# A 31 tap depthwise convolution split over three engines or over four

## The reference, cut to what matters

```python
def conformer_conv(h, w_pw1, b_pw1, w_dw, b_dw, ln_g, ln_b, w_pw2, b_pw2):
    a, gate = jnp.split(h @ w_pw1 + b_pw1, 2, axis=-1)
    y = a * jax.nn.sigmoid(gate)
    y = lax.conv_general_dilated(y, w_dw[:, None, :], window_strides=(1,),
                                 padding=[(CONV_K // 2, CONV_K // 2)],
                                 ...
                                 feature_group_count=CONV_W) + b_dw
    y = jax.nn.silu(layernorm(y, ln_g, ln_b))
    return y @ w_pw2 + b_pw2
```

## Time and profile before

| | |
|---|---|
| median of 3 executions | 3255.95 us (3248.94 to 3261.28) |
| the profiled execution | 3254.23 us |
| its span, first to last instruction | 3252.0 us |
| TensorE busy (matmul) | 2921.1 us, 90% |
| VectorE busy | 1574.0 us, 48% |
| ScalarE busy | 1086.2 us, 33% |
| GpSimd busy | 682.4 us, 21% |
| mean granted clock of TensorE | 0.908 of full speed |

### The profile page before, as it was taken

The page is one execution under the profiler, slowest core; times in us unless marked ns, Lnnn a source line. Parts: engine busy times, 40 slices in busy tenths (PEclk is TensorE's granted clock), DMA queues, the critical chain, the costliest instruction groups (busy, mean ns, idle before and its releaser), DMA issues. The chain is left out here.

```text
span 3252.0 us, 30964 instructions
## 1 busy us (share of the span) xinstructions
PE 2921.1 (90%) x12206; PEld 2206.4 (68%) x12206; DVE 1574.0 (48%) x2360; ACT 1086.2 (33%) x1578; POOL 682.4 (21%) x532
## 2 busy tenths in 40 slices
PE   6978589999999888899999897897999989899998
PEld 4855257888777633588887694355788866578886
DVE  5343536364342356364554425446555379743332
ACT  3222134343333334443334523333222231342223
POOL 6998910000000000000000000039995011000000
PEclk8975589999899889999998896788999899999999
DMA  5542212332212200123323230024554211123331
GB/s 165 165 144 93 85 58 78 97 98 89 67 60 72 78 1 1 52 85 97 97 88 101 76 97 13 1 65 136 170 173 136 72 52 60 44 74 96 97 97 52
DMA packets 284806, 274.66 MB, mean 84 GB/s; under 512 B 13473, under 2 KB 268727, under 8 KB 284407
## 3 DMA queue, kind: packets, MB, share of 16 engines
q1 hardware_dynamic: 266759, 210.47, 20.7%
q0 software_dynamic: 16864, 62.17, 5.8%
q10 hardware_dynamic: 1040, 0.07, 0.0%
HBM read 270.56 MB, written 2.10 MB: 84 GB/s over the span
## 5 line engine op out<-in xcount | busy, mean ns | idle before, releaser
L422 DVE TENSOR_TENSOR w_lo<-raw,w_hi 128x1024 fp32r<-128x1024 f32 x396 | 540.6, 1368 | 1110.8 <-ACT w_hi L418 1110.6
L1566 PE MATMUL G<-H_hi,w_hi 128*128 128x512 f32 (+1 forms) x2048 | 816.3, 399 | 84.6 <-DVE H_lo L330 37.4
L418 ACT ACTIVATE w_hi<-raw 128x1024 fp32r<-128x1024 f32 x396 | 418.4, 1057 | 1287.2 <-PE G L1566 1160.8
L1566 PE MATMUL G<-H_lo,w_hi 128*128 128x512 f32 (+1 forms) x2048 | 805.9, 393 | 0.0
L1566 PE MATMUL G<-H_hi,w_lo 128*128 128x512 f32 (+1 forms) x2048 | 805.1, 393 | 0.0
L1566 PEld LDWEIGHTS G<-H_hi,w_hi 128*128 128x128 f32 x2048 | 392.9, 192 | 185.6 <-issue 84.9
L1566 PEld LDWEIGHTS G<-H_lo,w_hi 128*128 128x128 f32 x2048 | 392.7, 192 | 83.4 <-issue 3.9
L1566 PEld LDWEIGHTS G<-H_hi,w_lo 128*128 128x128 f32 x2048 | 392.2, 191 | 81.9
L1566 PE MATMUL G<-hid_hi,w_hi 128*128 128x512 f32 x864 | 342.5, 396 | 4.6 <-DVE hid_lo L1227 3.9
L1566 PE MATMUL G<-hid_hi,w_lo 128*128 128x512 f32 x864 | 338.2, 391 | 0.0
L1566 PE MATMUL G<-hid_lo,w_hi 128*128 128x512 f32 x864 | 338.1, 391 | 0.0
(11 more groups left out here) (279 smaller groups left out, 3333.5 us busy)
## 6 DMA issues: line engine op xcount, KB each, us to landing
raw<-in_w_ff SPq DMA_DIRECT2D x128, 512.0 KB
mod_w<-in_w_mod POOLq DMA_DIRECT2D x112, 512.0 KB, 4.0
raw<-in_ffn_w_up SPq DMA_DIRECT2D x176, 256.0 KB
raw<-in_ffn_w_down SPq DMA_DIRECT2D x40, 512.0 KB
raw<-in_w_in SPq DMA_DIRECT2D x28, 512.0 KB
raw<-in_mlstm_w_in SPq DMA_DIRECT2D x24, 512.0 KB
raw<-in_kv_w SPq DMA_DIRECT2D x16, 512.0 KB
raw<-in_fox_w_qg SPq DMA_DIRECT2D x16, 512.0 KB
```

The lines of the kernel that those rows point to most:

```text
L418: act.activation(w_hi[:, j, :], raw[:, j, :], ACT.Copy).then_inc(hi_done, 1)
L422: dve.tensor_tensor(w_lo[:, j, :], raw[:, j, :], w_hi[:, j, :], ALU.subtract).then_inc(lo_done, 1)
L1566: mm = pe.matmul(G[:, 2 * p + m, 0:n], lw[:, k, ms], rh[:, t, 0:n], start=(t == 0 and q == 0), stop=(t == st["ktiles"] - 1 and q == 2), sk ...
```

## The change

TensorE keeps the last 7 of the 31 taps, VectorE the first 15. Nine taps, 15 to 23, are computed as products by ScalarE, `yp` times the tap's weight (a Copy with a scale per partition), into a ring of four tiles `tap_prod`; GpSimd adds the nine products of a group to `tap_sum` (a buffer of two) in eight chained additions. `total` on VectorE waits for these additions and adds `tap_sum` before it adds `M`. The diagonals of the next group are now built behind a group's additions.

```diff
-PE_TAPS = 10
-V_TAPS = CONV_K - PE_TAPS
+PE_TAPS = 7
+POOL_TAPS = 9
+V_TAPS = CONV_K - PE_TAPS - POOL_TAPS
...
+        tap_prod = at("tap_prod", 128 * K, [P, 4, T])
+        tap_sum = at("tap_sum", 136 * K, [P, 2, T])
...
                 for j in range(PE_TAPS):
-                    mm = pe.matmul(M[:, 2 + p, :], tap_diag[:, p, j, :], yp[:, p, V_TAPS + j:V_TAPS + j + T],
+                    mm = pe.matmul(M[:, 2 + p, :], tap_diag[:, p, j, :], yp[:, p, CONV_K - PE_TAPS + j:CONV_K - PE_TAPS + j + T],
                                    start=(j == 0), stop=(j == PE_TAPS - 1))
...
                 act.activation(S[:, p, :], G[:, 2 * p + 1, :], ACT.Sigmoid,
                                bias=VT[:, ds(g + (ROW["b_pw1_2"] + 8), 1)]).then_inc(glu_a, 1)
+                wait_read(act, "p_1", g)
+                for k in range(POOL_TAPS):
+                    n, j = POOL_TAPS * g + k, V_TAPS + k
+                    if n >= 4:
+                        old = n - 4
+                        act.wait_ge(cv_pp, (POOL_TAPS - 1) * (old // POOL_TAPS) + max(old % POOL_TAPS, 1))
+                    act.activation(tap_prod[:, n % 4, :], yp[:, p, j:j + T], ACT.Copy,
+                                   scale=vt("w_dw_2", 8 * j + g)).then_inc(cv_a, 1)
...
             def total(g, p):
 
                 dve.wait_ge(cv_pe, g + 3)
+                dve.wait_ge(cv_pp, (POOL_TAPS - 1) * (g + 1))
                 y = Y[:, ds(g, 1), :]
+                link(dve.tensor_tensor(y, y, tap_sum[:, p:p + 1, :], ALU.add))
                 dve.tensor_tensor(y, y, M[:, 2 + p:3 + p, :], ALU.add).then_inc(cv_d, 1)
...
             pool.wait_ge(chunk_used, used_after("s0_down3"))
             taps = VT[:, ROW["w_dw_2"]:ROW["w_dw_2"] + 8 * CONV_K].rearrange("p (j t) -> p j t", t=8)
-            for i in range(0, DT // 2):
-                for p in range(2):
-                    pool.wait_ge(cv_pe, i * 2 + (p + 1))
-                    pool.tensor_tensor(tap_diag[:, p], ident[:].unsqueeze(1).to_broadcast([P, PE_TAPS, P]),
-                                       taps[:, V_TAPS:CONV_K, ds(i * 2 + p, 1)].to_broadcast([P, PE_TAPS, P]),
-                                       ALU.mult).then_inc(cv_w, 1)
+            def diagonals(g):
+                p = g % 2
+                pool.wait_ge(cv_pe, g + 1)
+                pool.tensor_tensor(tap_diag[:, p], ident[:].unsqueeze(1).to_broadcast([P, PE_TAPS, P]),
+                                   taps[:, CONV_K - PE_TAPS:CONV_K, g:g + 1].to_broadcast([P, PE_TAPS, P]),
+                                   ALU.mult).then_inc(cv_w, 1)
+
+            def tap_sums(g):
+                acc = tap_sum[:, g % 2, :]
+                pool.wait_ge(cv_d, g + 1)
+                for k in range(1, POOL_TAPS):
+                    n = POOL_TAPS * g + k
+                    pool.wait_ge(cv_a, n + 1)
+                    if k == 1:
+                        one = pool.tensor_tensor(acc, tap_prod[:, (n - 1) % 4, :], tap_prod[:, n % 4, :], ALU.add)
+                    else:
+                        pool.wait_ge(cv_pp, (POOL_TAPS - 1) * g + k - 1)
+                        one = pool.tensor_tensor(acc, acc, tap_prod[:, n % 4, :], ALU.add)
+                    one.then_inc(cv_pp, 1)
+
+            diagonals(0)
+            for g in range(DT):
+                tap_sums(g)
+                if g < DT - 1:
+                    diagonals(g + 1)
```

More of the change, by code:

```diff
@@ L277, in build @@
         (rp_dma, tb_t, tb_r, tb_b, tb_mm, tb_e, ctx_dma, ct_t, ct_c, wsp_dma, sg_t, sg_w, sg_dg, sg_bc, sg_b, sg_v,
-         sg_r, sg_n, sg_m, glu_a, cv_d, cv_s, cv_m, cv_t, cv_y, cv_w, cv_pe, cv_v, fin_t, fin_m, fin_c) = [
+         sg_r, sg_n, sg_m, glu_a, cv_d, cv_s, cv_m, cv_t, cv_y, cv_w, cv_pe, cv_v, cv_a, cv_pp, fin_t, fin_m, fin_c) = [
             sem(k) for k in ("rp_dma tb_t tb_r tb_b tb_mm tb_e ctx_dma ct_t ct_c wsp_dma sg_t sg_w sg_dg sg_bc sg_b "
-                             "sg_v sg_r sg_n sg_m glu_a cv_d cv_s cv_m cv_t cv_y cv_w cv_pe cv_v fin_t fin_m "
+                             "sg_v sg_r sg_n sg_m glu_a cv_d cv_s cv_m cv_t cv_y cv_w cv_pe cv_v cv_a cv_pp fin_t fin_m "
                              "fin_c").split()]
```

## The result

The changed kernel took 3291.85 us (median of 4; 3289.87 to 3294.05) against 3256.31 us of the kernel before in the same comparison: ratio 1.0111, 95% interval 1.009 to 1.0132. It is 35.5 us slower, where 40.6 were forecast. The profiled execution has a span of 3288.0 us, 36.0 above that before.

The account below looks back on a forecast made before the run. VectorE, 19.2 us a group, was taken to bound stage p_1, TensorE a fraction behind. Terms +65.3, +9.8, +6.2, -31.8, -8.4 and -0.5 gave +40.6 us on 3255.95, so 3296.5 us; range 3276 to 3316.

Parts of the forecast that it names:

- Six taps leave VectorE: Stage p_1: VectorE does 13 taps a group in place of 19, 0.663 us each, 48 instructions fewer, -31.8 us.
- The addition of `tap_sum`: VectorE in p_1: one more addition a group behind a semaphore wait, 0.77 us, eight of them, +6.2 us.
- 64 additions: GpSimd in p_1: eight additions a group, each holding VectorE's two-SBUF-input instructions for 1.02 us, +65.3 us.
- Seven builds: GpSimd's diagonal builds of 896 columns, behind a group's additions, hold VectorE 1.4 us each, +9.8 us.
- `tensor_scalar` freed: VectorE's first `tensor_scalar` behind `yp` in p_1 no longer meets the diagonal builds, -8.4 us.
- Two engines full, VectorE deciding, TensorE a fraction behind: p_1 before the change: VectorE's 19.2 us a group decides the end, TensorE a fraction of a microsecond per group behind.
- TensorE idle 7.4 us a group: p_1 after the change: TensorE idles ahead of its taps; the lower clock then adds 2 us, hidden under VectorE.
- ScalarE's products hidden: p_1: nine products at 0.67 us, 6.0 a group; the ninth waits some 8 us after `yp`, hidden behind VectorE's taps.
- Eight long taps of 13 in each group: Sign in the profile after: VectorE's p_1 taps last 0.74 or about 1.75 us, eight of 13 the long ones.
- Rival A: No hindrance in p_1: TensorE's 16.9 us a group is the bound, 3233 us, faster; 6 in 100.
- Rival B: Half hindrance in p_1: additions cost VectorE 0.13 to 0.64 us each, within 16.3 us of now; 4 in 100.
- Rival C: GpSimd or TensorE's clock takes over in p_1: about +6 to +20 us on top, 3302 to 3316; 10 in 100.

Follow-up runs that it names:

- e3: Kernel before, plus eight chained GpSimd additions of 512 columns a group on a tile nobody uses; 3321.61 us against 3252.09, ratio 1.0223.
- e5: Changed kernel with GpSimd's additions 256 columns wide in place of 512, other half of the sum left out; 3256.88 us against 3252.09 of the kernel before.
- e1: Changed kernel with each of GpSimd's 64 additions one column wide, semaphores and ScalarE's products kept; 3230.32 us against 3250.36 of the kernel before.
- e2: Changed kernel with each GpSimd addition replaced by a 512 wide memset, which writes and does not read; 3226.36 us against 3250.36 of the kernel before.
- e4: Changed kernel, whole computation, with VectorE's two accumulators in PSUM; 3229.41 us against 3250.36 of the kernel before, run again 3236.51 against 3247.91.
- e8: Kernel before, its split of 10 and 21 taps kept, with VectorE's two accumulators in PSUM; 3252.87 us against 3252.09, ratio 1.0011.

## Why the prediction was right

By its own steps, each against the changed kernel's profile:

- *Six taps leave VectorE, -31.8 us*: held. 104 taps are left of 152, the free ones at 0.66 us.
- *The addition of `tap_sum`, +6.2*: measured +0.73 us a group, from a group's last tap to its next residual 2.83 us (2709.18 to 2712.01) where it was 2.10: +5.8.
- *64 additions, +65.3*: 1.70 us a tap in the group shown and 1.68 in the last, so 1.02 to 1.03 each, about 66 us. The row of the fold in another stage gave the price of an addition in this one to 2%. e3 shows it alone, e5 its dependence on width, e1 and e2 that neither ScalarE's reads nor the semaphores nor GpSimd's writes are the cause.
- *Seven builds, +9.8*: 1.45 us each, 10.1.
- *`tensor_scalar` freed, -8.4*: all eight at 545 to 548 ns, as forecast.
- *The stage*: the measured steps add up to +41.7 us, the forecast without the half microsecond ahead of the stage to +41.1, and the stage is 41.8 us longer. The medians differ by 35.5 us, whose interval (29 to 43 us) holds the forecast. In the two profiles the rest lies in the stages ahead, in code that is the same but for the shorter build. Executions of one kernel differ there by up to 16 us, so chance can explain it; that the change has no part in it is not shown.
- *Two engines full, VectorE deciding, TensorE a fraction behind*: close, but not exact. In the trace before, VectorE's groups are 19.2 us from the second to the fifth and 19.43 and 19.49 for the next two, TensorE's 19.5 all along: the first `tensor_scalar` waits for a build that TensorE's taps release, and this wait grew (from 1.79 to 2.09 us). At the end TensorE set the pace. The sum does not suffer, since it took the hindered `tensor_scalar` as measured in all six groups.
- *TensorE idle 7.4 us a group, less 2 us for a lower clock behind it, hidden*: 4.9 to 6.8 us between groups, taps 2.4 us longer, hidden.
- *ScalarE's products hidden*: yes, at 0.72 us each, not the 0.67 of the row taken; the fourth addition let the last product go at 2698.47, 7.8 us behind `yp`'s end (8 forecast).
- *Eight long taps of 13 in each group*: eight by additions, and a ninth by the build, which the sum had and the list of signs had not.

Rival A (no hindrance) did not happen in the changed kernel. e1 and e2, where the additions hold nothing, come within 3 us of its time. Rival B needed additions that mostly fall between taps or beside PSUM reads; all 64 met a tap. Rival C did not come: GpSimd's group is 15.3 us long (2692.14 to 2707.39), and TensorE's clock costs time that nobody waits for. What the forecast took from the Trainium skill ("SBUF — State Buffer", § Who interferes with whom) as the other sum, a lock held for the whole instruction, would have given 1.26 us an addition; all four widths show about 0.26 us less than the instruction lasts.

The prediction weighed the collision as a cost only. That the same rows hold its remedy (updates with a PSUM operand were free) stood in it as a detail; e4 shows that this detail is worth 54 us of the changed kernel's stage.

## What to carry to other kernels

Before work is given to GpSimd "for free", ask what VectorE does meanwhile: where both of its inputs are in SBUF and GpSimd reads SBUF, they take turns, and an addition moved over costs VectorE more (1.02 us) than the multiply-add it saves (0.66 us). A `tensor_scalar` from SBUF to SBUF, with one input, is held too (1.59 and 1.48 us in e3, 0.55 and 0.48 alone). Give VectorE's instruction one operand in PSUM and the two run side by side (e4); where TensorE is as full as VectorE this gains nothing by itself (e8). The price can be read beforehand in any stage where both are busy: compare the pitch of VectorE's instructions there with their pitch alone.

## What the runs showed of the hardware that was not expected

In e2, where memsets come ahead of it, the build of diagonals is the one that waits. GpSimd:

```profile
2679.64 4.36 POOL L1546 TENSOR_TENSOR tap_diag<-ident,VT 128x896 f32<-128x896 f32 x1
```

VectorE in the same stretch (L1413 taps, L1394 the addition of `tap_sum`):

```profile
2679.70 0.75 DVE L1413 SCALAR_TENSOR_TENSOR S<-yp,VT,S 128x512 f32<-128x512 f32 x1
...
2681.69 0.75 DVE L1413 SCALAR_TENSOR_TENSOR Y<-yp,VT,Y 128x512 f32<-128x512 f32 x1
2682.47 2.07 DVE L1394 TENSOR_TENSOR Y<-Y,tap_sum 128x512 f32<-128x512 f32 x1
```

The build starts at 2679.64, 0.06 us ahead of a tap, and yet four taps in a row pass 0.66 us apart; only when VectorE pauses behind its last tap (2682.47) does it get in, and it lasts 4.36 us in place of 1.70. In the other six groups the build starts about 0.35 us ahead of a tap, and again four pass. In the changed kernel the build at 2705.24, behind an addition, holds the very next tap; so it does behind additions of one column (e1), and behind idle time it holds the next residual (e8, 4.52 us at 2667.74). So the strict turns of one to one belong to GpSimd instructions that read, and one that reads behind some that only write can be held off by VectorE for several of its instructions. What in the memsets brings this about was not settled.
